# Modulation weights paired by shift and scale in one block, and query-rank weights loaded and split earlier

## What is computed

```python
mod = (silu(c) @ w_mod + b_mod).reshape(6, D)      # shift, scale, gate, shift, scale, gate
h = rms_norm(x, g_norm1) * (1 + mod[1]) + mod[0]   # for latent and for context tokens
p = h @ w_in                                       # 512 query-rank, 320 kv, 3 x 1024 neighbourhood columns
```

## Time and profile before

| | |
|---|---|
| runs | 2093.07 us median, 2092.68 to 2094.48 |
| profiled execution | 2088.43 us, span 2086.5 us |
| TensorE matmul | 1938.2 us busy, 93% of the span |
| VectorE | 832.6 us, 40% |
| ScalarE | 427.1 us, 20% |
| GpSimd | 174.4 us, 8% |
| DMA | 602.78 MB, mean 289 GB/s |
| mean granted TensorE clock | 0.987 |

### The profile page before, as it was taken

One profiled execution on the slowest core, in us unless ns is written; L12 is line 12 of the kernel. 1 busy time (PEld: TensorE's weight loads), 2 busy tenths in 40 slices (PEclk: granted clock), 3 DMA queues, 4 the chain that ended last, 5 costly groups with the idle time before them and its releaser, 6 DMA issues.

```text
span 2086.5 us, 25707 instructions
## 1 busy us (share of the span) xinstructions
PE 1938.2 (93%) x10114; PEld 1231.2 (59%) x10114; DVE 832.6 (40%) x1723; ACT 427.1 (20%) x1141; POOL 174.4 (8%) x402
## 2 busy tenths in 40 slices
PE   4899999999999999989996999998989999898988
PEld 2578788878877777768885533433435353443433
DVE  5557877773245555534444131221303021121303
ACT  4223223122145555532222000000000000000000
POOL 0003112011133322200000000000000000000000
PEclk9999999999999999999997999999999999999999
DMA  9937888783122111132228999999999999999998
GB/s 403 421 141 270 325 294 291 270 282 138 46 102 86 45 44 44 43 134 81 81 81 353 395 419 429 427 427 428 427 428 427 428 427 427 428 428 427 426 428 355
DMA packets 77079, 602.78 MB, mean 289 GB/s; under 512 B 7568, under 2 KB 25232, under 8 KB 33568
## 3 DMA queue, kind: packets, MB, share of 16 engines
q1 hardware_dynamic: 64224, 591.11, 70.0%
q10 hardware_dynamic: 12592, 8.98, 1.3%
q0 software_dynamic: 144, 1.05, 0.1%
HBM read 584.32 MB, written 16.79 MB: 288 GB/s over the span
## 4 chain that ended last, share of the span: by engine, by line
PE 50%; DMA 11%; DVE 2%; ACT 2%; issue 1%; POOL 0%; DVEq 0%; ACTq 0%
DMA arena<-in_w_gate_up 10%; PE SM L1115 7%; PE TM L1115 7%; PE SM L1145 6%; PE TM L1145 5%; PE TR L1064 3%; PE MJ L1064 2%; PE TM L919 1%; PE SM L885 1%; PE SN L1102 1%; DMA wor<-in_w_out 1%; PE MJ L817 1%; PE MJ L821 1%; PE SM L890 1%; PE SM L960 1%
## 5 line engine op out<-in xcount | busy, mean ns | idle before, releaser
L1115 PE MATMUL SM<-arena 128*64 128x512 f32 x1024 | 245.0, 598 | 47.2 <-DMA arena<-in_w_gate_up 46.7
L1115 PE MATMUL TM<-arena 128*64 128x512 f32 x1024 | 242.7, 592 | 0.0
L1683 DVE SCALAR_TENSOR_TENSOR arena<-arena,csil 128x512 f32<-128x512 f32 x240 | 180.3, 751 | 46.7 <-DMA arena<-in_w_mod 38.3
L1115 PEld LDWEIGHTS SM<-arena 128*64 128x64 f32 x1024 | 71.0, 136 | 191.4 <-issue 190.5
L1115 PEld LDWEIGHTS TM<-arena 128*64 128x64 f32 x1024 | 78.6, 137 | 141.1 <-issue 141.1
L1145 PE MATMUL SM<-arena 128*64 128x512 f32 x512 | 117.8, 609 | 1.5 <-DVE arena L2011 1.5
L1145 PE MATMUL TM<-arena 128*64 128x512 f32 x512 | 116.9, 599 | 0.0
L1203 ACT ACTIVATE wh<-wr 128x2048 fp32r<-128x2048 f32 (+1 forms) x32 | 58.7, 1835 | 192.4 <-PE TN L720 148.8
L1931 DVE TENSOR_TENSOR arena<-cst,rope_t 128x512 f32<-128x512 f32 x8 | 5.5, 692 | 230.3 <-PE MJ L1088 230.3
L718 PE MATMUL SM<-wh,h_hi 128*128 128x512 f32 (+1 forms) x224 | 89.2, 398 | 7.8 <-DVE h_lo L1631 7.8
L1413 ACT CAST y_hi<-arena 128x512 fp32r<-128x512 f32 x32 | 19.8, 619 | 367.7 <-DVE arena L1967 367.7
(11 more groups left out here) (327 smaller groups left out, 3488.1 us busy)
## 6 DMA issues: line engine op xcount, KB each, us to landing
arena<-in_w_gate_up SPq DMA_DIRECT2D x128, 2048.0 KB, 16.3
arena<-in_w_down SPq DMA_DIRECT2D x64, 2048.0 KB, 25.5
arena<-in_w_mod SPq DMA_DIRECT2D x96, 1024.0 KB, 5.5
wr<-in_w_na SPq DMA_DIRECT2D x24, 1024.0 KB, 7.0
wor<-in_w_out SPq DMA_DIRECT2D x8, 2048.0 KB, 7.9
xT<-in_tokens_t SPq DMA_DIRECT2D x4, 1536.0 KB, 12.6
arena<-in_w_qkv SPq DMA_DIRECT2D x8, 640.0 KB, 5.4
wr<-in_w_qa SPq DMA_DIRECT2D x4, 1024.0 KB, 11.9
```

Of the source, the lines that this page charges most:

```text
L1115: mm = pe.matmul(GU[b][64 * e:64 * e + CAP, :], xsT[:, k, 64 * e:64 * e + CAP], w[:, 2 * (b // 2) + e, (b % 2) * NB:(b % 2 + 1) * NB], sta ...
L1683: ve.scalar_tensor_tensor(acc, row, c, acc, ALU.mult, ALU.add).then_inc(mod_step, 1)
```

## The change

1. **Host layout.** The first 4096 columns of `w_mod` are reordered so that block `pos` holds 256 shift columns and the 256 scale columns of the same two row groups (2 pos and 2 pos + 1). `MOD_ORDER` is gone. Sizes and numbers of transfers stay.
2. **Modulation in twos.** After each block VectorE computes the multiplier and the parts of two row groups. The latent half comes first, and the low part of the first group stands behind two scalings. ScalarE's order follows.
3. **Waits of TensorE.** A query-rank step waits for the latent `h_lo` alone. A new wait for all 32 low parts stands ahead of the kv tiles of the context tokens.
4. **TensorE's order.** In each block two quarters, a step, two quarters, a step, columns; in the last block the columns come ahead of the step. Three steps follow them.
5. **Weights.** `w_qa` piece 0 is fetched ahead of all modulation pieces, and pieces 1, 2 and 3 after blocks 0, 2 and 4 (before, pieces 0 to 3 came after blocks 0, 2, 4 and 6). ScalarE and VectorE split piece 0 ahead of the root of the token squares, and piece w + 1 after the row groups of block 2w.

```diff
-MOD_ORDER = [0, 4, 1, 5, 2, 6, 3, 7]
+MOD_K = KD // (2 * MODB)
+W_AHEAD = {0: 1, 2: 2, 4: 3}
...
 # SyncE
-            for pos, b in enumerate(MOD_ORDER):
+            load_w(0)
+            for pos in range(2 * MODB):
...
-                    sp.dma_start(mod_a[n % MOD_RING], mod_piece(b, kq)).then_inc(ma_in[n % MOD_RING], 16)
-                if pos % 2 == 0:
-                    load_w(pos // 2)
+                    sp.dma_start(mod_a[n % MOD_RING], mod_piece(pos, kq)).then_inc(ma_in[n % MOD_RING], 16)
+                if pos in W_AHEAD:
+                    load_w(W_AHEAD[pos])
             load_w(4)
...
 # TensorE
-                pe.wait_ge(lo_set, 2 * k + 2)
+                pe.wait_ge(lo_set, 4 * (k // MOD_K) + k % MOD_K + 1)
...
             mod_columns(0)
...
+            for pos in range(1, 2 * MODB):
+                k = MOD_K * (pos - 1)
                 mod_quarter(pos, 0)
                 mod_quarter(pos, 1)
                 qa_step(k)
                 mod_quarter(pos, 2)
                 mod_quarter(pos, 3)
+                if pos + 1 < 2 * MODB:
+                    qa_step(k + 1)
+                    mod_columns(pos)
+                else:
+                    mod_columns(pos)
+                    qa_step(k + 1)
+            qa_step(KD - 2)
+            qa_step(KD - 1)
...
                     if tile == 0:
                         pe.wait_ge(w_low, w + 1)
+                    if s == LT:
+                        pe.wait_ge(lo_set, 2 * KD)
...
 # ScalarE
+            sc.wait_ge(ss_step, 1)
+            high(0)
             sc.wait_ge(rb_full, AT)
             sc.copy(rstd_b[:, 0:SEQ], RSTD_BANK)
             sc.copy(rstd_b[:, SEQ:TOK], TR[:, 0:CTX]).then_inc(rb_copied, 1)
-            high(0)
-            for k in range(KD):
+            for pos in range(2 * MODB):
                 for c, (lo, hi) in enumerate(((0, SEQ), (SEQ, TOK))):
-                    sc.wait_ge(h_part, 2 * k + c + 1)
-                    sc.activation(h_hi[:, k, lo:hi], xT[:, k, lo:hi], ACT.Identity, bias=modcol[:, k, c:c + 1]).then_inc(hi_set, 1)
-                if k % 4 == 3:
-                    high(k // 4 + 1)
+                    for i in range(MOD_K):
+                        k = MOD_K * pos + i
+                        sc.wait_ge(h_part, 4 * pos + 2 * c + i + 1)
+                        sc.activation(h_hi[:, k, lo:hi], xT[:, k, lo:hi], ACT.Identity, bias=modcol[:, k, c:c + 1]).then_inc(hi_set, 1)
+                if pos % 2 == 0:
+                    high(pos // 2 + 1)
...
 # VectorE
             def mod_columns(pos):
+                two = slice(MOD_K * pos, MOD_K * pos + MOD_K)
                 ve.wait_ge(ma_col, pos + 1)
+                ve.tensor_tensor(modcol.rearrange("p (s k) c -> p s k c", s=2)[:, :, two, :],
+                                 MJ[:, 0:8].rearrange("p (s k c) -> p s k c", s=2, k=MOD_K),
+                                 bcol.rearrange("p (s k) -> p s k", s=2)[:, :, two].unsqueeze(3).broadcast_to([P, 2, MOD_K, 2]),
+                                 ALU.add).then_inc(ma_free, 1)
...
             ve.tensor_copy(rowsum[0:1, SEQ:TOK], TR[0:1, 0:CTX]).then_inc(ss_step, 1)
+            low(0)
...
+            def scale_part(pos, c, i):
+                k, (lo, hi) = MOD_K * pos + i, HALVES[c]
+                ve.scalar_tensor_tensor(xT[:, k, lo:hi], xT[:, k, lo:hi], mul1[:, k, c:c + 1], rstd_b[:, lo:hi],
+                                        ALU.mult, ALU.mult).then_inc(h_part, 1)
+            def low_part(pos, c, i):
+                k, (lo, hi) = MOD_K * pos + i, HALVES[c]
+                ve.wait_ge(hi_set, 4 * pos + 2 * c + i + 1)
+                ve.scalar_tensor_tensor(h_lo[:, k, lo:hi], xT[:, k, lo:hi], modcol[:, k, c:c + 1], h_hi[:, k, lo:hi].bitcast(F32),
+                                        ALU.add, ALU.subtract).then_inc(lo_set, 1)
             for pos in range(2 * MODB):
+                two = slice(MOD_K * pos, MOD_K * pos + MOD_K)
+                scale = slice(KD + MOD_K * pos, KD + MOD_K * pos + MOD_K)
                 take_mod(pos)
                 mod_columns(pos)
-                if pos % 2:
-                    apply_mod(pos // 2)
-                else:
-                    low(pos // 2)
-            low(4)
+                ve.wait_ge(ma_free, pos + 1)
+                ve.scalar_tensor_tensor(mul1[:, two, :], modcol[:, scale, :], 1.0, g1[:, two].unsqueeze(2).broadcast_to([P, MOD_K, 2]),
+                                        ALU.add, ALU.mult).then_inc(mul_set, 1)
+                ve.wait_ge(mul_set, pos + 1)
+                if pos == 0:
+                    ve.wait_ge(rb_copied, 1)
+                scale_part(pos, 0, 0)
+                scale_part(pos, 0, 1)
+                low_part(pos, 0, 0)
+                scale_part(pos, 1, 0)
+                low_part(pos, 0, 1)
+                scale_part(pos, 1, 1)
+                low_part(pos, 1, 0)
+                low_part(pos, 1, 1)
+                if pos % 2 == 0:
+                    low(pos // 2 + 1)
...
 # host
+    paired = np.arange(2 * D).reshape(2, 2 * MODB, NB // 2).swapaxes(0, 1).reshape(-1)
+    w_mod = g["w_mod"][:, np.concatenate([paired, np.arange(2 * D, 6 * D)])]
```

More of the change, by code:

```diff
@@ L764, in _ @@
                 mod_quarter(pos, 2)
-                qa_step(k + 1)
                 mod_quarter(pos, 3)
[L767 to L775, removed]
+                if pos + 1 < 2 * MODB:
[6 more added lines that the diff above has]
+            qa_step(KD - 1)
             def turn(n):
@@ L1587, in mod_columns, with low @@
             def mod_columns(pos):
-                b = MOD_ORDER[pos]
+                two = slice(MOD_K * pos, MOD_K * pos + MOD_K)
                 ve.wait_ge(ma_col, pos + 1)
-                ve.tensor_tensor(modcol[:, 4 * b:4 * b + 4, :], MJ[:, 0:8].rearrange("p (a b) -> p a b", b=2),
-                                 bcol[:, 4 * b:4 * b + 4].unsqueeze(2).broadcast_to([P, 4, 2]), ALU.add).then_inc(ma_free, 1)
+                ve.tensor_tensor(modcol.rearrange("p (s k) c -> p s k c", s=2)[:, :, two, :],
+                                 MJ[:, 0:8].rearrange("p (s k c) -> p s k c", s=2, k=MOD_K),
+                                 bcol.rearrange("p (s k) -> p s k", s=2)[:, :, two].unsqueeze(3).broadcast_to([P, 2, MOD_K, 2]),
+                                 ALU.add).then_inc(ma_free, 1)
+            def low(w):
+                ve.wait_ge(w_high, w + 1)
+                n = KQ * (Q_RANK if w < W_KV else KV_N if w < W_NA else NB)
+                ve.tensor_tensor(w_lo[w % 3][:, 0:n], w_raw[w % 3][:, 0:n], w_hi[w % 2][:, 0:n].bitcast(F32), ALU.subtract).then_inc(w_low, 1)
             ve.wait_ge(ss_step, 1)
@@ L1603, in _ @@
                 ve.tensor_scalar(diag[tile % 2], ident, x_rstd[:, tile:tile + 1], None, ALU.mult).then_inc(diag_set, 1)
[L1605 to L1609, removed]
             HALVES = ((0, SEQ), (SEQ, TOK))
[L1613 to L1632, removed]
@@ L2125, in laid_out @@
         "consts": np.concatenate([consts[n].astype(np.float32) for n, _ in CONST_SIZES], axis=1),
-        "w_mod": to_rows(g["w_mod"].reshape(D, 6 * MODB, NB).swapaxes(0, 1), 6 * MODB, 4),
+        "w_mod": to_rows(w_mod.reshape(D, 6 * MODB, NB).swapaxes(0, 1), 6 * MODB, 4),
         "b_mod": np.asarray(inputs["b_mod"]),
```

## The result

The kernel after takes 2076.99 us in the median of 4 runs (2076.26 to 2080.8) against 2092.88 us of the kernel before (4 runs, 2092.47 to 2094.48): ratio 0.9931, 95% interval 0.992 to 0.9942, so 15.9 us (12 to 17) less. Three later comparisons, one on chip 12 and two on chip 1, give more runs of both: before 2091.00, 2091.70 and 2090.75 us (23, 28 and 23 runs), after 2077.89 us on chip 12 and 2079.27 us on chip 1 (6 runs each, ratios 0.9938 [0.9923, 0.9953] and 0.9941 [0.9929, 0.9953]). Pooled, these 74 runs of before have a median of 2091.2 us and a mean granted clock of 0.9858; the 16 runs of after, the first four among them, have 2078.8 us and 0.9897. The gain of the pools is 12.4 us.

The account below looks back on a forecast made before the run. It took TensorE's own order as the bound at the stage's end, with data binding only around 48 us. A 10.45 us gain less 1.57 for one half-clock stretch gave 8.9, so 2084.2 us from 2093.07, range 2080.5 to 2090.5.

Parts of the forecast that it names:

- The stage: From first modulation columns to first 320-column matmul: forecast to end at 126.31 instead of 136.76 us, before the clock charge.
- The chain: TensorE's sequence of columns, hand-overs, steps and quarters in the stage: 11.50 us a block, 10.45 us less at full clock.
- both covers for the moved splits: Slack for weight splits on VectorE: 0.7 us before the token squares, 1.1 us behind even blocks; cost taken as 0.
- the one for the transfers: Slack for reordered transfers: modulation piece (2,1) lands about 50.5, wanted at 51.7 us; cost 0, bounds 0 and 2.1.
- The half-clock term: One stretch of TensorE at half clock charged in the stage, since some idling remains in every block: 1.57 us.
- The base: Forecast subtracted its gain from the median 2093.07 us, taking the gain from a profiled execution of 2088.43 us.
- The rule that I weighed: Bursts alternating with waits are throttled at each wait; by it 7 hand-overs would leave the sum near nothing.
- B: Columns come late as the split behind even blocks runs into the next copy: 2088.2 us; chance 12%.
- C: Every hand-over ends in a half-clock stretch, 11.0 us in all: 2093.6 us, no change; chance 6%.
- E: Clock falls twice in each block, after hand-over and after paired quarters, 22.0 us: 2104.6 us, slower; chance 3%.
- D: The gain is given back later, by the state of the ring or expert weights: 2093 us; chance 6%.
- F: No half clock and shorter hand-overs than the chain, data as floor: about 2080.5 us; chance 7%.

Follow-up runs that it names:

- e12: The kernel after, unchanged, third time, on chip 1: 2079.27 us, ratio 0.9929 to 0.9953 against before.
- e4: The kernel after with 4 unused small matmuls ahead of each block's first step, filling its idling: 2079.11 us, ratio 0.9923 to 0.9954 against before.
- e1: The kernel before again, no edit: 2091.72 us, ratio 0.9995 to 1.0012 against before.
- e3: The kernel after again, unchanged, on chip 12: 2077.89 us, ratio 0.9923 to 0.9953 against before.
- e7: The kernel after, but all four scalings come first and steps wait for both token halves: 2093.78 us, ratio 1.0002 to 1.0021 against before.
- e9: The kernel after with steps waiting for both token halves, plus 7 unused small matmuls filling each hand-over's idling: 2086.93 us, ratio 0.9972 to 0.999 against before.
- e10: The kernel before with only the latent-first order and steps waiting for the latent half alone: 2087.18 us, ratio 0.9973 to 0.999 against before.
- e5: The kernel before with only the earlier fetches and splits of the weights: 2095.77 us, ratio 1.0008 to 1.003 against before.
- e6: The kernel after with the weights fetched and split as before: 2086.05 us, ratio 0.9957 to 0.9978 against before.
- e2: The kernel before with its hand-over idling filled by 7 or 14 unused small matmuls: 2087.19 us, ratio 0.9966 to 0.9987 against before.
- e8: The kernel after with three quarters ahead of a block's first step: 2079.81 us, ratio 0.9929 to 0.996 against before.
- e11: The kernel after with three quarters ahead of first steps, last block's four quarters and step before columns, kv split last: 2076.65 us, ratio 0.9917 to 0.9941.

## Why the prediction was wrong

**The stage was right.** Unit times, hand-over and sum came out: idling 0.93 to 1.02 us where 1.12 was forecast, 11.43 and 11.51 us per block against 11.50, columns 6 and 7 at 107.58 and 117.04 against 107.40 and 116.92, stage end 126.45 against 126.31. The chain gave 10.45 us less before the charge for clock; the two traces differ by 10.63. Later waits stayed nearly what they were the earlier trace rows, and both covers for the moved splits and the one for the transfers held (e12's trace has one wait of 0.4 us for a transfer).

**The half-clock term failed.** The step is "I charge one stretch, 1.57, since some idling remains in every block". There was none in any of three traces of the kernel after, and filling the remaining idling (e4) changed nothing. Without this charge the sum gives 2082.6, still 5.6 us above the measured 2077.0. So the step accounts for 1.6 of the 7.0 us between the 8.9 forecast and the 15.9 measured.

**The base was one execution.** The sum also took the profiled execution of before for a usual one. It had a clock of 0.987 and was 4.6 us short of the median, which was stated as something "which I can't place in a stage". A part can be placed: the clock lost in this stage changes from run to run, e1's trace lost 1.6 us more there, and the mean clock of the 74 runs is 0.9858. The prediction counted three stretches of 1.57; the clock of 0.84 over the last 21.86 us is a shortfall of 3.5 us, twice that of the third part (1.8), so the last one was worth two. That didn't enter the sum. Both traces of before together give a stage of 99.3 and the three of after 87.8: 11.5 us, 0.8 more than the traced pair. If e1's trace is the usual one, it is 1.6 more; two traces can't tell. The clock term and the base together explain 2.4 to 3.2 of the 7.0 us, and a gain of 11.3 to 12.1 us. That is the 12.4 of the pools within about 1 us.

**The rest of the 15.9.** The remaining 3.8 to 4.6 us stay open. The first comparison, of four runs each, has before at 2092.9 and after at 2077.0; the pools have 2091.2 and 2078.8. Of these 3.5 us, the 1.8 of the kernel after are in part the clock's: its first four runs had 0.989, 0.990, 0.991 and 0.991, against 0.9897 in the pool, and its times follow the clock (e3). The other 1.7, of before, can be chance or the chip; the clocks of those runs aren't on record. Half-clock windows behind the stage come and go too: from 560 to 600 us the clock is 1.00 and 0.91 in the two traces of before, 0.96, 1.00 and 1.00 in the three of after. What follows the stage took 1949.7 and 1951.3 us in the traces of before, and 1952.5, 1954.0 and 1951.8 in those of after. So no trace shows the stage's whole gain at the end of the program, and only the medians of the pools do. Which later stage lost it, and whether the change has a hand in it, no run here tells.

**The rule that I weighed.** The Trainium skill's section on oscillation ("TensorE: Matmul & The Clock Gate", "HAM oscillation — how this bites in real kernels") was read as speaking against the change, since it makes 7 hand-overs of 4. The page's own case has waits of about 3 to 5 us for transfers, so it says less against waits of 1.1 us than I took from it. The runs turn it round: it speaks against what the change removes. e7 shows its mechanism (1.9 to 2.0 us of idling per hand-over, clock down after five of seven), e9 that filling cures it. But the number of waits is not what counts: 7 waits of up to 1.0 us cost no clock in three traces, and before, three of 2.0 to 3.9 us and one for a transfer cost it three times in each of two traces.

**Which part carries it.** I had priced the latent-first wait as one term of the hand-over. It is what the rest stands on: without it the change is a loss of 2.1 us (e7), alone it brings 3.6 (e10). The early weights, which I priced at nothing, cost 4.1 us alone (e5) and are worth 6.8 by the medians of the same chip and 5.9 in the stage once blocks are paired (e6), for then the first step has nothing else to wait for. "Cost 0" was right for the change as a whole and says nothing of the part. Paired blocks alone, with neither of the other two, were not run. Rivals B, C and E did not occur. Of D, a gain given back later, the traced pair shows 2.8 us and the pools show little. F's "no half clock" did occur, with the chain as forecast, and the 2077.0 is below F's 2080.5 without being explained by it.

## What to carry to other kernels

A wait of TensorE between bursts has two prices, its length and the clock that it may bring down, and the second can be the larger: here 1 us more at a hand-over cost 2.5 where the clock fell. When a profile shows half-clock stretches beside a removable wait, compare the clock of every timed run before taking one trace's count as usual, and test the waits by filling them with matmuls whose result nobody reads, which keeps the order and all waits and takes away the idling. Parts of such a change don't add up; each can be a loss alone.

## What the runs showed of the hardware that I had not expected

Useless matmuls in idle stretches made a kernel faster: 3.8 us in e2, 6.9 us by the medians in e9 against e7. In otherwise equal blocks, idling of 0.5 to 1.0 us never lowered the granted clock (three traces of seven hand-overs each), nor did waits of 1.4 us for transfers (e8, e11); 1.9 to 2.0 us did at five of seven hand-overs (e7). In the first blocks of the old order, quarters and columns alone without a query-rank step, the clock fell with no wait above 0.9 us (e10). Runs of the kernel after differ by 7 us, and follow their granted clock (0.991 at 2076.3 to 2077.0 us, 0.987 at 2083.57). The same hand-over that kept its clock in one execution lost it in another (the earlier trace rows and e1, second window: 24.04 at 1.00 and 25.63 at 0.93).
